# Spreading the gates: three of four groups of first one-hot rows made by GpSimd, and the key row read from PSUM

## What is computed

```python
best, pos = lax.top_k(cand, K)
expert = jnp.take_along_axis(cand_idx, pos, axis=-1)
gate = jax.nn.softmax(best, axis=-1)
ue = u[expert]
h = jax.nn.gelu(jnp.einsum("thkd,td->thk", ue, xb).astype(jnp.float32), approximate=False)
w = (gate * h).astype(xb.dtype)
ve = v[expert]
return jnp.einsum("thk,thkd->td", w, ve)
```

## Time and profile before

| | us |
|---|---|
| median of 3 runs | 5826.04 |
| lowest, highest | 5822.16, 5826.12 |
| the profiled execution, its own time | 5824.08 |
| its span in the trace | 5822.6 |
| the gates' stage, from the first comparison to the last result of ACT | 2908 to 3275 |

### The profile page before, as it was taken

The page is one execution under the profiler, slowest core; times in us unless marked ns, Lnnn a source line. Parts: engine busy times, 40 slices in busy tenths (PEclk is TensorE's granted clock), DMA queues, the critical chain, the costliest instruction groups (busy, mean ns, idle before and its releaser), DMA issues. The chain is left out here.

```text
span 5822.6 us, 71414 instructions
## 1 busy us (share of the span) xinstructions
PE 4962.2 (85%) x24196; PEld 3981.3 (68%) x24196; DVE 3859.4 (66%) x7482; ACT 1516.5 (26%) x2312; POOL 2345.1 (40%) x1600
## 2 busy tenths in 40 slices
PE   7999994554888789965177499999999999999999
PEld 6888883441444367455165388888888888888888
DVE  2000004883777512289799688888888888888887
ACT  3111103553444421100066422222222222222221
POOL 4222202551000032035500166666666666666664
PEclk9999996777999899977599799999999999999999
DMA  3222211103111042220035677777777777777776
GB/s 122 89 81 81 85 40 58 36 9 129 39 54 41 16 176 94 76 66 0 23 115 173 204 266 244 238 238 244 243 245 237 246 249 244 237 237 247 242 243 216
DMA packets 350400, 862.42 MB, mean 148 GB/s; under 512 B 26920, under 2 KB 161864, under 8 KB 350024
## 3 DMA queue, kind: packets, MB, share of 16 engines
q1 hardware_dynamic: 229328, 415.33, 22.0%
q0 software_dynamic: 120992, 446.13, 22.0%
HBM read 733.33 MB, written 126.71 MB: 148 GB/s over the span
## 5 line engine op out<-in xcount | busy, mean ns | idle before, releaser
L2152 PE MATMUL e_ph<-e_x,e_u 128*128 128x512 f32 (+1 forms) x6144 | 1385.9, 364 | 59.5 <-DVE e_x L2217 44.0
L2152 PEld LDWEIGHTS e_ph<-e_x,e_u 128*128 128x128 f32 x6144 | 1129.5, 189 | 231.5 <-issue 36.4
L2174 PE MATMUL e_po<-e_v,e_w 128*128 128x512 f32 x4608 | 1184.3, 392 | 5.2 <-DVE e_w L2238 5.2
L2174 PEld LDWEIGHTS e_po<-e_v,e_w 128*128 128x128 f32 x4608 | 859.2, 188 | 155.2 <-issue 5.8
L310 PE MATMUL proj_acc<-xn,w_tile 128*128 128x512 f32 x3600 | 706.0, 358 | 3.7 <-POOL xn L350 3.7
L310 PEld LDWEIGHTS proj_acc<-xn,w_tile 128*128 128x128 f32 x3600 | 599.1, 188 | 110.7 <-POOL xn L350 4.1
L2249 DVE TENSOR_TENSOR e_acc<-e_acc,e_po 128x512 f32<-128x512 f32 x768 | 517.4, 680 | 173.8 <-PE e_po L2174 173.8
L2074 ACT ACTIVATE e_act<-e_ph 128x512 f32<-128x512 f32 (+1 forms) x256 | 139.6, 545 | 1806.2 <-PE e_ph L2152 1806.2
L2266 DVE SCALAR_TENSOR_TENSOR e_tok<-e_row,e_slot,e_tok 128x1024 f32<-128x1024 f32 x384 | 586.0, 1539 | 2.4 <-DMA e_tok<-h_tok_dram 2.4
L2255 DVE SCALAR_TENSOR_TENSOR e_row<-e_row,e_tok 128x1024 f32<-128x1024 f32 x384 | 574.4, 1502 | 9.6 <-DMA e_row<-in_u_rows,expert_tok 9.6
L2108 POOL TENSOR_TENSOR e_u<-e_u_raw,e_u 128x1024 fp32r<-128x1024 f32 x128 | 380.5, 2972 | 415.1 <-ACT e_u L2057 415.1
(11 more groups left out here) (299 smaller groups left out, 6473.4 us busy)
## 6 DMA issues: line engine op xcount, KB each, us to landing
e_u_raw<-in_u_exp SPq DMA_DIRECT2D x128, 512.0 KB
e_v_raw<-in_v_exp SPq DMA_DIRECT2D x128, 512.0 KB
gates_dram<-g_out SPq DMA_DIRECT2D x7, 8192.0 KB, 25.6
e_g<-gates_dram SPq DMA_DIRECT2D x128, 448.0 KB, 3.9
feat_dram<-proj_out POOLq DMA_DIRECT2D x50, 640.0 KB, 5.7
w_raw<-in_w_feat SPq DMA_DIRECT2D x50, 512.0 KB, 4.8
raw<-feat_dram SPq DMA_DIRECT2D x32, 640.0 KB, 5.8
mx_gate<-feat_dram SPq DMA_DIRECT2D x16, 640.0 KB, 4.0
```

The costliest lines, as they stand in the source:

```text
L2152: ins = nc.tensor.matmul(ph[q % 2][:, 0:tn], u[b][j][:, kk, :], xs[m][:, kk, t0:t0 + tn], start=(i == 0), stop=(i == 3 * DC - 1))
L2174: ins = nc.tensor.matmul(out, w[b][j][:, blk * P:(blk + 1) * P], v[2 * odd + b][m][:, half * HALF:(half + 1) * HALF], start=(n == 0 and (f ...
```

## The change

`g_now` gets four buffers in place of two. A PSUM tensor `g_key_ps` is added, and DVE copies the key row into it once at the start of the stage. DVE's comparisons read the key row from there. For groups 0, 1 and 2 of each round DVE no longer makes `g_first`; POOL makes it, by twelve TENSOR_SCALARs of 128 x 128 a round, each a comparison of `g_key` (in SBUF) with one token's first key. POOL's program is written out for all 56 rounds in place of a loop. PE waits for one more semaphore, `pooled[p]`, for those three groups. Group 3 stays as it was but for the key row's place. DVE's loop runs over four rounds at a time.

```diff
     STEP = GRP * RING
     ROUNDS = P // STEP
     ROWS = 3
+    STAGES = 4
+    POOLED = 3
...
-        now = [sb(f"g_now{b}", [P, ROWS, STEP]) for b in range(2)]
+        now = [sb(f"g_now{b}", [P, ROWS, STEP]) for b in range(STAGES)]
...
+        key_ps = ctx.enter_context(nc.psum_tensor("g_key_ps", [P, KEYS], F32))
...
+        pooled = [sem(f"g_pooled{b}") for b in range(POOLED)]
...
-                def round_of(n, h, begun):
-
-                    if begun:
-                        pool.wait_ge(marked[RING - 1], n - 1)
-                    nc.gpsimd.tensor_copy(now[h][:], r[:, :, bass.ds(n * STEP, STEP)]).then_inc(staged, 1)
+                def stage(n):
+
+                    if n >= STAGES:
+                        pool.wait_ge(marked[RING - 1], n - STAGES + 1)
+                    nc.gpsimd.tensor_copy(now[n % STAGES][:], r[:, :, n * STEP:(n + 1) * STEP]).then_inc(staged, 1)
+
+                def firsts(n):
+
+                    pool.wait_ge(staged, n + 1)
+                    for p in range(POOLED):
+                        if n:
+                            pool.wait_ge(summed[p], n)
+                        for j in range(GRP):
+                            at = p * GRP + j
+                            ins = nc.gpsimd.tensor_scalar(first[p][:, j, :], key[:], now[n % STAGES][:, 0, at:at + 1], None, ALU.is_equal)
+                        ins.then_inc(pooled[p], 1)
 
                 for n in range(2):
-                    round_of(n, n, False)
-                with pool.Fori(1, DB * ROUNDS // 2) as i:
-                    for h in range(2):
-                        round_of(2 * i + h, h, True)
+                    stage(n)
+                for n in range(DB * ROUNDS):
+                    if n + 2 < DB * ROUNDS:
+                        stage(n + 2)
+                    firsts(n)
...
-                with dve.Fori(0, DB * ROUNDS // 2) as i:
-                    for h in range(2):
-                        n = 2 * i + h
+                nc.vector.tensor_copy(key_ps[:], key[:]).then_inc(key_kept, 1)
+                dve.wait_ge(key_kept, 1)
+                with dve.Fori(0, DB * ROUNDS // STAGES) as i:
+                    for h in range(STAGES):
+                        n = STAGES * i + h
                         dve.wait_ge(staged, n + 1)
                         for p in range(RING):
                             dve.wait_ge(summed[p], n)
-                            nc.vector.tensor_tensor(first[p][:], key[:].unsqueeze(1).broadcast_to([P, GRP, KEYS]),
-                                                    now[h][:, 0, p * GRP:(p + 1) * GRP].unsqueeze(2).broadcast_to([P, GRP, KEYS]), ALU.is_equal)
+                            if p >= POOLED:
+                                nc.vector.tensor_tensor(first[p][:], key_ps[:].unsqueeze(1).broadcast_to([P, GRP, KEYS]),
+                                                        now[h][:, 0, p * GRP:(p + 1) * GRP].unsqueeze(2).broadcast_to([P, GRP, KEYS]), ALU.is_equal)
                             for j in range(GRP):
                                 at = p * GRP + j
-                                ins = nc.vector.tensor_scalar(second[p][:, j, :], key[:], now[h][:, 1, at:at + 1], now[h][:, 2, at:at + 1],
+                                ins = nc.vector.tensor_scalar(second[p][:, j, :], key_ps[:], now[h][:, 1, at:at + 1], now[h][:, 2, at:at + 1],
                                                               ALU.is_equal, ALU.mult)
                             ins.then_inc(marked[p], 1)
...
                         pe.wait_ge(marked[p], n + 1)
+                        if p < POOLED:
+                            pe.wait_ge(pooled[p], n + 1)
                         pe.wait_ge(kept[p], n)
```

More of the change, by code:

```diff
@@ L1843, in spread_gates @@
         acc = [ctx.enter_context(nc.psum_tensor(f"g_acc{b}", [P, GRP, KEYS], F32)) for b in range(RING)]
-        r_in, key_done, staged = sem("g_r_in"), sem("g_key_done"), sem("g_staged")
+        key_ps = ctx.enter_context(nc.psum_tensor("g_key_ps", [P, KEYS], F32))
+        r_in, key_done, key_kept, staged = sem("g_r_in"), sem("g_key_done"), sem("g_key_kept"), sem("g_staged")
+        pooled = [sem(f"g_pooled{b}") for b in range(POOLED)]
         marked = [sem(f"g_marked{b}") for b in range(RING)]
```

## The result

The changed kernel takes 5864.51 us (median of 6 runs, 5860.94 to 5869.0) against 5826.08 for the kernel before (median of 6, 5822.16 to 5827.85): 38 us slower, ratio 1.0067, 95% interval 1.0054 to 1.0080. The forecast was 5778, so faster. The direction is rival C's and the time is near C's 5853, but, as the runs show, the cause is not C's.

What follows compares the result with a forecast made beforehand. DVE was taken to bound the stage; its round falls from 6.51 to 5.64 us, 0.87 x 56 = 48.7, less 0.4 for the copy to PSUM: 48 us, giving 5778. The range was 5722 to 5808.

Steps and rivals of the forecast that it cites:

- rival C: DVE and POOL still wait for each other via per-partition operands and POOL's key read: 0.54 a comparison, 5853 us; chance 0.07.
- What bounds the kernel before: In the gates' stage DVE, busy without a gap, sets the time: 6.51 us a round, 56 rounds, 364.5 us.
- The TENSOR_TENSORs taken from DVE and the price of PSUM: DVE's round: three TENSOR_TENSORs fewer save 1.80 us; 16 TENSOR_SCALARs reading PSUM cost 0.06 more each, 0.96 us.
- Rivals A: DVE's comparisons cost no more from PSUM, 0.25 each: 5736 us, at best 5722; chance 0.20.
- rival D: A DVE instruction reading PSUM pays a second fixed part: TENSOR_SCALAR 0.375, round 6.66, 8 us more, 5834; chance 0.04.
- What POOL gets: POOL's twelve comparisons at 0.34 and one copy at 0.16: 4.2 us a round, hidden behind DVE's 5.64.
- Do DVE and POOL disturb each other?: With the key of DVE's comparisons in PSUM, nothing is charged to either engine for contention.
- Rival B: POOL becomes the bound, still faster: a comparison at 0.50, round 6.16, saving 20 us, 5806; chance 0.09.
- POOL's written-out program: Loading POOL's unrolled instructions as it runs: taken as 0, at most three landings of 4 us, 10 us.
- The tail: After the stage's last ACT result: last 8 MB go out in 25.6 us, next stage 26.7 after issue; unchanged.
- The range: Whole kernel time from 5722 (DVE's PSUM comparisons cost no more, best case) to 5808 (POOL as bound, still faster).

Runs made afterwards that it cites:

- the half alone: Changed kernel with buffers aligned, DVE reading the key row from PSUM and POOL making no first rows, against the kernel before: 5880.52 us against 5826.43, ratio 1.0095.

## Why the prediction was wrong

- *What bounds the kernel before*: right. DVE set the rounds; with two and with no groups on POOL the rounds followed DVE's sum (6.30 and 7.49 us against 6.24 and 7.50).
- *The TENSOR_TENSORs taken from DVE and the price of PSUM*: right. A comparison costs 0.06 more: its step is 0.319, forecast as 0.315, and the half alone cost 54 us. Rivals A and D are out. By the figures of the Trainium skill that rival D names (VectorE: DVE Perf Modes, The TRN2 errata) the estimate is 0.13 us more for a comparison from PSUM. The run with that half alone does not agree: 54 us are 0.06 for each of its 896.
- *What POOL gets*: here it failed, in the price of one comparison and its upper bound. "From above" I had put the two-input TENSOR_TENSOR of 128 columns, 0.399, with 0.06 for the operand, 0.46, and I took 0.34 because the comparison has one input. It measured 0.58, above the bound. On POOL the TENSOR_SCALAR is the dearer kind at both widths on record: at 128 columns it lasts 0.592 against 0.399, at 512 its step is 1.54 against 1.00. A bound from another operation was no bound, and the row that the middle came from (the select) was the furthest off. The term is 12 x 0.58 + 0.19 = 7.15 us a round in place of 4.2, and past 0.53 a comparison the sign turns, as the text had it. With 0.58 in it the prediction's own sum gives 7.15 x 56, 36 us more than before.
- *Do DVE and POOL disturb each other*: right as to the PSUM rows. Rival C named a time near the measured one (5853), but for a cause that two runs refute. Rival B had the mechanism, POOL as the bound, and stopped at 0.50. So the one right direction, C's, came with a wrong cause.
- *POOL's written-out program*: taken as nothing, and right. POOL has no gap, and the two instruction queues moved 38 and 48 packets against 38 and 42.
- *The tail*: "the change leaves it" was wrong by 4.8 us. The buffers' place in the memory is a part of the change too.
- *The range* (5722 to 5808) was built on the same bound; all of its upper part hung on a comparison of at most 0.50. The text named this as what would make it wrong, and gave "slower" a chance of only 0.09.

## What to carry to other kernels

Before work is moved to another engine, price the very instruction there: operation, kind of operands and width. If no row shows it, the bounds are wide on both sides, and a count of twelve a round multiplies the error; a short list of such instructions ahead of the stage costs one run and led here to a version 147 us faster than the change. In this stage GpSimd did better with few wide two-input products than with many narrow TENSOR_SCALARs. One input of VectorE in PSUM kept the two engines apart; for a wide TENSOR_TENSOR it cost nothing (0.60 either way), for a 128-column TENSOR_SCALAR 0.06 us. And look where a new buffer pushes the ones behind it.

## What the runs showed of the hardware

- GpSimd's TENSOR_SCALAR in f32 costs 0.27 us and 2.5 ns a column (128, 256 and 512 columns, start to start), with an immediate as with a per-partition value, and at 128 columns for a comparison as for a product. Its TENSOR_TENSOR of 512 columns, a subtraction, costs 1.00 us in all.
- VectorE's per-partition operands cost 0.06 us each: the 128-column TENSOR_SCALAR from PSUM costs 0.20 without one, 0.26 with one and 0.32 with two, start to start.
- VectorE's and GpSimd's TENSOR_TENSORs of 512 columns, both with two SBUF inputs, last 1523 and 1421 ns where they run side by side, and 677 and 1040 with one of VectorE's inputs in PSUM.
- A store of 8 MB from rows of 512 bytes takes 25.6 us from a buffer that begins on a multiple of 512 bytes, and 30.3 to 30.4 from one 384 bytes further.
